# Moving the first normalisation's squares and column sums in a two-block transformer kernel

## The reference, cut to what matters

```python
def rmsnorm(x, g):
    xf = x.astype(jnp.float32)
    y = xf * lax.rsqrt(jnp.mean(xf * xf, axis=-1, keepdims=True) + NORM_EPS)
    return (y * g.astype(jnp.float32)).astype(x.dtype)

def token_mixer(x, g_pre, ...):
    h = rmsnorm(x, g_pre)
    proj = h @ w_in
    u, q, k, v, o, gi, gf, ga, gb = jnp.split(proj, IN_SPLITS, axis=-1)
    y_a = jax.nn.gelu(s5_ssm(u, lam_re, lam_im, b_re, b_im, c_re, c_im, d, log_dt))
    ...
```

## Time and profile before

| | us |
|---|---|
| median of 3 runs | 1443.49 |
| the runs | 1443.34 to 1444.8 |
| the profiled execution, its own time | 1443.67 |
| its span from the first to the last instruction | 1441.9 |
| PE busy | 1423.2 (99%) |
| DVE busy | 842.8 (58%) |
| ACT busy | 607.5 (42%) |
| POOL busy | 305.2 (21%) |

### The profile page before, as it was taken

One profiled execution on the slowest core, in us unless ns is written; L12 is line 12 of the kernel. 1 busy time (PEld: TensorE's weight loads), 2 busy tenths in 40 slices (PEclk: granted clock), 3 DMA queues, 4 the chain that ended last, 5 costly groups with the idle time before them and its releaser, 6 DMA issues.

```text
span 1441.9 us, 23164 instructions
## 1 busy us (share of the span) xinstructions
PE 1423.2 (99%) x9151; PEld 1228.8 (85%) x9151; DVE 842.8 (58%) x1267; ACT 607.5 (42%) x924; POOL 305.2 (21%) x287
## 2 busy tenths in 40 slices
PE   8999999999999999999999999999999999999999
PEld 8999999999998988998997777767678888888887
DVE  6888654457465543553355637898877534344355
ACT  6552577743343321222224446666655314233230
POOL 2660334300115622660363000002103000000000
PEclk9999999999999999999999999999999999999999
DMA  5212112124312232233224132111133222323221
GB/s 207 69 66 80 54 59 74 59 89 148 103 60 75 101 116 88 88 102 103 88 87 141 51 103 73 59 40 49 50 118 118 97 97 92 103 92 104 95 95 66
DMA packets 35848, 128.34 MB, mean 89 GB/s; under 512 B 4084, under 2 KB 4468, under 8 KB 35632
## 3 DMA queue, kind: packets, MB, share of 16 engines
q1 hardware_dynamic: 34608, 122.18, 25.2%
q10 hardware_dynamic: 864, 4.33, 0.8%
q0 software_dynamic: 288, 0.57, 0.1%
HBM read 124.92 MB, written 2.10 MB: 88 GB/s over the span
## 4 chain that ended last, share of the span: by engine, by line
PE 85%; DVE 9%; POOL 2%; ACT 2%; issue 1%; DMA 0%; SPq 0%; DVEq 0%; ACTq 0%; POOLq 0%
PE ps L1947 70%; PE ps L2356 3%; DVE rot L970 2%; PE ps L2186 1%; POOL phase_tmp L1765 1%; PE ps L2452 1%; DVE w_lo L966 1%; PE ps L2475 1%; PE ps L2414 1%; DVE rot L1222 1%; PE ps L2465 1%; PE ps L2006 1%; POOL phase L1765 1%; PE ps L2300 1%; PE ps L2298 1%
## 5 line engine op out<-in xcount | busy, mean ns | idle before, releaser
L966 DVE TENSOR_TENSOR w_lo<-w_raw,w_hi 128x1024 fp32r<-128x1024 f32 (+2 forms) x225 | 294.2, 1309 | 147.6 <-ACT w_hi L392 146.8
L1947 PE MATMUL ps<-h_hi,w_hi 128*128 128x512 f32 (+3 forms) x1168 | 331.5, 333 | 3.7 <-DVE qk L970 1.8
L1947 PE MATMUL ps<-h_hi,w_lo 128*128 128x512 f32 (+3 forms) x1168 | 321.0, 324 | 0.0
L1947 PE MATMUL ps<-h_lo,w_hi 128*128 128x512 f32 (+3 forms) x1168 | 320.8, 324 | 0.0
L392 ACT ACTIVATE w_hi<-w_raw 128x1024 fp32r<-128x1024 f32 (+2 forms) x226 | 231.4, 1032 | 167.3 <-PE ps L1947 156.0
L1947 PEld LDWEIGHTS ps<-h_hi,w_hi 128*128 128x128 f32 x1168 | 196.1, 188 | 32.9 <-issue 11.8
L1947 PEld LDWEIGHTS ps<-h_lo,w_hi 128*128 128x128 f32 x1168 | 195.8, 188 | 19.8 <-issue 2.9
L1947 PEld LDWEIGHTS ps<-h_hi,w_lo 128*128 128x128 f32 x1168 | 195.9, 188 | 17.8
L1947 PE MATMUL ps<-f_hi,w_hi 128*128 128x256 f32 (+1 forms) x488 | 129.5, 319 | 0.0
L1947 PE MATMUL ps<-f_hi,w_lo 128*128 128x256 f32 (+1 forms) x488 | 129.5, 319 | 0.0
L1947 PE MATMUL ps<-f_lo,w_hi 128*128 128x256 f32 (+1 forms) x488 | 129.4, 319 | 0.0
(11 more groups left out here) (381 smaller groups left out, 2339.8 us busy)
## 6 DMA issues: line engine op xcount, KB each, us to landing
w_raw<-w_units SPq DMA_DIRECT2D x227, 512.0 KB, 3.2
x<-x_t ACTq DMA_DIRECT2D x1, 2112.0 KB, 8.4
out<-out_tile SPq DMA_DIRECT2D x7, 256.0 KB, 2.0
x<-x_t ACTq DMA_DIRECT2D x3, 528.0 KB, 9.2
x<-x_t ACTq DMA_DIRECT2D x2, 264.0 KB, 4.5
consts<-consts SPq DMA_DIRECT2D x1, 320.0 KB, 6.9
b_step<-ssm_b SPq DMA_DIRECT2D x1, 256.0 KB, 10.5
c_step<-ssm_c SPq DMA_DIRECT2D x1, 256.0 KB, 11.5
```

The lines of the kernel that those rows point to most:

```text
L966: Dv.do(v.tensor_tensor(wlo[:, s % RING, 0:w], raw[:, s % RING, 0:w], f32(whi[:, s % RING, 0:w]), ALU.subtract), lo_ready)
L1947: ins = mm(o, wt[:, s % RING, w], xt[:, kx, c0:c0 + n], start=(b == 0 and a == 0), stop=(b == len(blocks) - 1 and a == 2))
```

## The change

Four things are moved. Nothing is computed that was not computed before.

1. ACT writes all eight `h_hi` first, then `w_hi` of unit 1, and then the squares of tiles 0 to 3 only.
2. POOL makes the squares of tiles 4 to 7 (`tensor_tensor`, x times x), behind its memsets and ahead of the operation on `c_step`.
3. PE waits for nothing but its operands in unit 0. Both `four_sums` stand behind the second block of unit 1, and `parts_sum` behind the fourth.
4. DVE copies the partial sums ahead of `w_lo` of unit 2, and makes the diagonal tables behind unit 0's eviction, ahead of `step_sizes`.

```diff
@@ scalar
                 if m == KT - 1:
                     split_hi(1)
-                for k in (range(KT - 2, KT) if m == KT - 1 else range(m, m + 1) if m < KT - 2 else ()):
-                    A.do(dn.activation(sq0[k][:, :], x[:, k, :], ACT.Square), sem("tile_sq"))
+            for m in range(KT // 2):
+                dn.activation(sq0[m][:, :], x[:, m, :], ACT.Square).then_inc(sem("tile_sq"), 2)
@@ vector
-                if norm < 5:
+                if 0 < norm < 5:
                     dve.wait_ge(sem("stat_part"), PRE.index(norm) + 1)
                     Dv.do(v.tensor_copy(shape(sq[1]), sums), sem("part_copied"))
...
-            dve.wait_ge(sem("consts_in"), 16)
-            Dv.do(v.tensor_reduce(eye32[:, :], ident.rearrange("p (g c) -> p c g", g=4), AX.X, A_))
-            Dv.fence()
-            for t in range(CT):
-                ts(dmat[:, t, :], eye32[:, :], col("ssm_d", t), 0.0, M, A_, sem("d_ready"))
+            def skip_diagonal():
+
+                dve.wait_ge(sem("consts_in"), 16)
+                Dv.do(v.tensor_reduce(eye32[:, :], ident.rearrange("p (g c) -> p c g", g=4), AX.X, A_))
+                Dv.fence()
+                for t in range(CT):
+                    ts(dmat[:, t, :], eye32[:, :], col("ssm_d", t), 0.0, M, A_, sem("d_ready"))
...
+                if n == 0:
+                    dve.wait_ge(sem("stat_part"), 1)
+                    Dv.do(v.tensor_copy(two(sq[1][:, :]), PS[:, 4:6, 0:HALF]), sem("part_copied"))
                 if n - 2 not in E_AFTER and turned != 0 and not weighs:
                     split_lo(n + LOOK)
...
                 if n == 0:
+                    skip_diagonal()
                     step_sizes()
@@ gpsimd
             Po.do(g.memset(c_pow[:, :, :, :, :], 0.0), sem("zeros"))
+            for m in range(KT // 2, KT):
+                if m in X_PARTS:
+                    pool.wait_ge(sem(f"x_in{X_PARTS.index(m)}"), 16)
+                tt(sq0[m][:, :], x[:, m, :], x[:, m, :], M, sem("pool_sq"))
@@ tensor
-            pe.wait_ge(sem("consts_in"), 16)
             def first_after(b):
                 if b == FIRST // P - 1:
                     pe.wait_ge(lo_ready, 1)
-                if b % 4 == 3:
-                    four_sums(0, T1, b, sq0)
+            def second_after(b):
+                if b == 1:
+                    pe.wait_ge(sem("consts_in"), 16)
+                    pe.wait_ge(sem("tile_sq"), KT)
+                    pe.wait_ge(sem("pool_sq"), KT // 2)
+                    four_sums(0, T1, 3, sq0)
+                    four_sums(0, T1, 7, sq0)
+                if b == 3:
+                    parts_sum(0, T1)
...
-                    unit(n, 0, hhi, hlo, halves(n), after=lambda b: parts_sum(0, T1) if b == 0 else None)
+                    unit(n, 0, hhi, hlo, halves(n), after=second_after)
```

## The result

The changed kernel takes **1447.98 us** (median of 9 runs, 1447.84 to 1448.1), the kernel before 1443.49: 4.5 us slower, ratio 1.0031, 95% interval 1.0022 to 1.0039. The forecast was 1448.8, slower by over 0.2%, range 1445.5 to 1450.5.

What follows compares the result with a forecast made beforehand. The bound was taken to be the chain of waits from `rs` over DVE and POOL to 115.73, not PE; 0.5 gained, 2.12, 1.02 and 2.7 lost: 5.3 us on 1443.49, 1448.8 us, range 1445.5 to 1450.5.

Steps and rivals of the forecast that it cites:

- The chain from `rs` to 115.73 has no slack: From the factor `rs` over DVE and POOL to PE's wait ending at 115.73: a delay of `rs` arrives whole.
- ACT gains 0.5 us, not 3.2, since x isn't there: ACT in the entry: without squares between, high halves end only 0.5 us earlier, as x's last part lands at 13.45.
- PE's sums in unit 1, +2.12: PE in unit 1: from `w_lo` to `parts_sum` 4.94 us in place of 2.82, so `rs` comes 2.12 later.
- The tables, +1.02: DVE's diagonal tables, behind unit 0's eviction: 1.02 us, formerly within the 2.82 from `w_lo` to `parts_sum`, now come on top.
- GpSimd's squares, +2.7: POOL's squares beside DVE's `h_lo`: engines take turns, 0.95 us per square, making `w_lo` of unit 1 2.7 later.
- The `c_step` row: POOL's operation at 15.26 beside two `h_lo` cost them at most 0.1 us, so squares could cost next to nothing.
- The upper bound of that term: POOL's squares: a slow first operation, as the 1.06 us copy at 48.81, would add up to 0.9 us.
- No hold-up: Rival: POOL's squares don't hold DVE up in the entry; +2.6 us, 1446.1; chance 0.22.
- x in time: Rival: x lands up to 2 us sooner in the entry, only the tables remain; +0.9, 1444.4; chance 0.05.
- The clock: Rival: PE, idle about half of 9 to 19 us, is then granted 1.2 GHz; +10.2, 1453.7; chance 0.04.

Runs made afterwards that it cites:

- e3: Kernel before with PE's part alone: both `four_sums` behind unit 1's second block, `parts_sum` behind its fourth; 1445.51 us, ratio 1.0015.
- e4: Kernel before with the diagonal tables alone moved behind unit 0's eviction; 1444.12 us, +0.83.
- e9: Changed kernel without GpSimd's four squares, the sums reading the squares of tiles 0 to 3 again (output wrong); 1446.04 us.
- e12: e11 with its first small `step_sizes` operations moved behind GpSimd's memset; 1440.33 us, ratio 0.9977 against the kernel before.
- e1: Changed kernel with the diagonal tables alone moved back to their old place behind `w_lo` of unit 1; 1447.04 us.
- e6: Kernel before, DVE reordered: copy of sums right behind unit 1's `w_lo`, unit 2's `w_lo` behind the eviction, tables behind the last `b_step`; 1443.59 us.
- e5: Changed kernel, with weights of units 1 to 3, ssm_b and ssm_c issued only after x tiles 4 and 5 land; 1447.26 us.
- e7: Kernel before with e6's tables and unit 2's `w_lo`, POOL squaring tiles 0 to 3 before its memsets, sums in unit 0, earlier copy; 1445.76 us.
- e10: e6 with unit 2's `w_lo` moved behind the copy of the sums, into DVE's wait for the root; 1442.57 us.
- e11: e10 with the small `step_sizes` operations spread into DVE's waits of the entry; 1441.96 us.
- e2: Changed kernel with GpSimd squaring tiles 0 to 3 and ACT tiles 4 to 7; 1446.98 us.
- e8: e7 with e5's wait, holding back weights until x tiles 4 and 5 land; 1444.15 us.

## Why the prediction was right

The direction and the mechanism held, and the size nearly: 4.5 us of the 5.3 forecast, the difference lying mostly in one term, GpSimd's squares. Point by point:

- **The chain from `rs` to 115.73 has no slack.** Right: a shift of 4.4 at `step_sizes` was 4.37 at the rotations and at PE's wait, and 4.4 in the span. e3, e4 and e9 moved by what their links moved, and e12 shows from the other side that PE takes over once the chain is some 3 us shorter.
- **ACT gains 0.5 us, not 3.2, since x isn't there.** Right: the last wait for x ended at 13.37 (13.5 said). In e9, where nothing else disturbs, `w_lo` of unit 1 is ready at 16.6, against 17.0 said. This term was not run by itself. What is left for it when the others are taken from the total is -0.6 (4.49 - 2.22 - 0.94 - 1.94), or -0.2 with e1 and e9 each against the kernel before beside it (4.49 - 2.22 - 0.74 - 1.74). The 0.5 is thus borne out by the traces, and by the times only in its sign.
- **PE's sums in unit 1, +2.12.** Right: e3 measured +2.22. The 4.94 us behind `w_lo` were 5.2, since two blocks between operations of another shape take 1.67 to 1.72, not 1.45; the two sums are 1.92, less than the 2.04 said.
- **The tables, +1.02.** Right in size: 0.7 to 0.9 by e1, 0.83 by e4. The step counted the tables as part of 2.82 us that went away, and that was right for the sum. I then read it in e4's expectation as time that would be saved at the old place, which was wrong: ACT's `w_hi` of unit 2 is what ends last there.
- **GpSimd's squares, +2.7.** The mechanism was right, the term too large: 1.7 to 1.9 by e9 (2.2 between the two profiles). The turn was taken as 0.95 from additions of 525 and 512 columns that started inside a DVE operation; it measured 0.72 (1.49 from start to start less 0.77), and the nearer row, 0.84, would have been the better choice. Three turns less by 0.23 are 0.7 us of the difference between 19.7 said and 18.75 measured for the end of `w_lo`; the rest is the first square, through at 12.38 and not at 12.7.
- **The `c_step` row**, which the prediction set against the turns, showed a small price and not none. In e12, where the same operation of 0.89 starts at 14.92, the `h_lo` beside it takes 0.90 in place of 0.77. Why an operation of 256 columns with one input costs DVE 0.13 and a square of 528 columns with two inputs 0.72 was not tested.
- **The upper bound of that term**, a slow first operation of POOL, had a wrong reason: e6 shows the 1.06 us at 48.81 to be a wait beside DVE's `w_lo`. The row was one more sign for the turns, and I had read it as something else.
- **The rivals.** No hold-up (1446.1) is what e9 gives without the squares (1446.04), and the changed kernel isn't there. x in time fell: e5 hastens x and keeps 3.85 us. The clock stayed at 1.00 in all nine runs of the changed kernel, where PE idled for a third of the time from 8 to 20 us, not for half of it. It fell in e7, and cost 1.4 to 3 us there. That the changed kernel was spared by more than chance isn't shown.

The Trainium skill, "SBUF — State Buffer", section "Who interferes with whom", says that a VectorE operation with two SBUF inputs contends with a GpSimd operation that reads SBUF and not with one that only writes it, and that a `tensor_scalar` can run in a two-port mode, in which it contends with GpSimd too. The traces agree on the first two: `h_lo` beside a square takes 1.57, `h_lo` beside the memset 0.77. The third fits the small `tensor_scalar` beside the memset, 1.98, but no run shows the mode that it ran in.

## What to carry to other kernels

Before moving work to an engine that idles, look at what the others do in the same microseconds: GpSimd had 6 us free, but every square that took a full turn there cost DVE 0.72 us on the chain. When a page says that one engine is 98% busy, follow the chain of waits all the same, since a short stretch of small operations on another engine can hold it, and ask of each of them whether it needs to be there: putting 14 of the 18 small operations of 0.2 us into waits that DVE had anyway gave 2.3 us (e12 against e10), which no shuffling of squares and sums did. And where an operation seems to cost its own time in one place, see what it covers: moved away, it can leave a wait of the same length.

## What the runs showed of the hardware

- **Turns.** A GpSimd square of 128x528 takes 1.07 us when it needn't wait (e7, at 4.37 and 6.53; beside the second, DVE's `w_lo` of 256 columns, begun 0.03 us later, took 1.31 in place of 0.43). In a row with `h_lo` it is 1.53 with 1.49 from start to start; the two engines alternate, operation by operation, in every run that has both.
- **A small `tensor_scalar` waits for the rest of a memset of GpSimd**: 1.98 in place of 0.17 when it started 2.4 us into one of 4.37 (e11), 0.18 once it stands behind it (e12), while `h_lo`, with two inputs, passes the same memset in its usual 0.77.
- **The granted clock can fall for about 4 us, in some executions only.** In the profiled execution of e7 PE was busy for 0.94 of the 2 us from 10 to 12 and was then granted 0.59 and 0.56 for 4 us, near the level of 1.2 GHz, and 1.00 again from 16. In that of e2 it was busy for 0.97 there, and was granted 0.70 and 0.50 until 16. But in that of e8 it was busy for the same 0.97 and kept 1.00; and in that of e1 the clock fell elsewhere, to 0.56 and 0.58 from 120 to 124, behind a stretch from 116 to 120 with PE busy for 2.21 of 4 us, while the kernel before, busy for 0.27 of the 2 us from 114 to 116, kept 1.00. The runs of e7 at a mean clock of 1.0 took 1444.10 to 1444.35, those at 0.999 1445.6 to 1445.8, those at 0.998 1446.9 to 1447.2. In e2 it cost less: 1447.02 in the median at 0.999, 1446.88 at 1.0. e4, e6, e8 and e11 had such runs too, and the kernel before had two of 15 beside e12 (1444.92 and 1445.26 beside 1443.39); the changed kernel had none in nine, e12 none in eleven. What decides between executions of one kernel stays open.
